# Hybrid mixer block: the delta rule's front moved to the end of its own turn, its levels spread, the first convolution tap on ScalarE

## The reference, cut to what matters

```python
qkv = jax.nn.silu(causal_depthwise_conv(concat([dq, dk_, dv_]), dn_conv_w))   # 4 taps per channel
q = l2_normalize(cq) * DN_KEY_DIM ** -0.5;  k = l2_normalize(ck);  v = cv
decay = exp(where(causal, gcum[..., :, None] - gcum[..., None, :], -inf))
a_mat = einsum('bnhid,bnhjd->bnhij', k_beta, k) * decay * strict
sol = triangular_solve(eye + a_mat, [v * beta, k_beta * exp(gcum)])            # unit lower triangular
qk = einsum('bnhid,bnhjd->bnhij', q, k) * decay
# scan over chunks: v_new = u - w @ state;  o = q_dec @ state + qk @ v_new;  state = state * d + k_dec^T @ v_new
o_dn = rms_norm(o) * gain * silu(z)
```

## Time and profile before

| | |
|---|---|
| median of three runs | 1932.82 us |
| time of the profiled execution | 1932.75 us |
| its span | 1930.9 us |
| busy: PE, PEld, DVE, ACT, POOL | 99%, 83%, 66%, 53%, 3% |
| granted TensorE clock, mean | 0.998 of full speed |

### The profile page before, as it was taken

How to read it: one execution, slowest core, us unless ns; L and a number is a source line. 1 busy time by engine, 2 the same in 40 slices (tenths; PEclk the granted TensorE clock), 3 DMA queues, 4 the chain that set the end, 5 groups by cost and what they waited for, 6 DMA issues and landing times.

```text
span 1930.9 us, 27778 instructions
## 1 busy us (share of the span) xinstructions
PE 1908.9 (99%) x9545; PEld 1607.1 (83%) x9545; DVE 1273.1 (66%) x2261; ACT 1023.4 (53%) x2068; POOL 49.6 (3%) x80
## 2 busy tenths in 40 slices
PE   9999999999999999999999999999999999999997
PEld 7888888888888888888888788888888888888886
DVE  6658888888888756565665786555555555555555
ACT  4446665666566655455444554545444444444443
POOL 1000000000000000000000000000000000000000
PEclk9999999999999999999999999999999999999999
DMA  8666555455535557566566456555565565655552
GB/s 315 207 159 190 135 136 136 132 129 132 145 117 129 181 173 245 195 202 202 189 236 206 153 198 197 194 192 182 191 196 185 186 195 181 226 202 196 196 194 89
DMA packets 204178, 349.62 MB, mean 181 GB/s; under 512 B 6768, under 2 KB 73024, under 8 KB 203088
## 3 DMA queue, kind: packets, MB, share of 16 engines
q1 hardware_dynamic: 200704, 334.00, 52.6%
q0 software_dynamic: 3264, 14.47, 4.7%
q10 hardware_dynamic: 144, 0.26, 0.0%
HBM read 344.32 MB, written 2.10 MB: 179 GB/s over the span
## 4 chain that ended last, share of the span: by engine, by line
PE 89%; DVE 5%; issue 2%; ACT 2%; DMA 1%; DVEq 0%; ACTq 0%; POOL 0%; SPq 0%; POOLq 0%
PE dense L602 23%; PE dense L604 23%; PE dense L603 23%; PE dense L590 8%; PE dense L592 4%; PE chain L760 1%; DVE lo L1422 1%; DMA raw<-in_w_in_dram 1%; PE chain L842 1%; ACT hi L1077 1%; PE chain L1027 0%; PE chain L852 0%; PE chain L719 0%; PE chain L860 0%; DVE AT L1680 0%
## 5 line engine op out<-in xcount | busy, mean ns | idle before, releaser
L1422 DVE TENSOR_TENSOR lo<-raw,hi 128x512 fp32r<-128x512 f32 x1252 | 849.2, 690 | 518.9 <-ACT hi L1077 516.5
L1077 ACT ACTIVATE hi<-raw 128x512 fp32r<-128x512 f32 x1252 | 773.2, 630 | 620.2 <-PE dense L604 596.9
L602 PE MATMUL dense<-hi,xs 128*128 128x512 f32 x1376 | 539.7, 392 | 1.7 <-DVE xs L1970 1.1
L604 PE MATMUL dense<-lo,xs 128*128 128x512 f32 x1376 | 535.9, 389 | 0.0
L603 PE MATMUL dense<-hi,xs 128*128 128x512 f32 x1376 | 535.5, 389 | 0.0
L590 PE MATMUL dense<-xs,hi 128*128 128x512 f32 x1024 | 380.3, 410 | 1.0
L602 PEld LDWEIGHTS dense<-hi,xs 128*128 128x128 f32 x1376 | 258.4, 188 | 55.3 <-DVE xs L1970 2.0
L604 PEld LDWEIGHTS dense<-lo,xs 128*128 128x128 f32 x1376 | 258.3, 188 | 54.2
L603 PEld LDWEIGHTS dense<-hi,xs 128*128 128x128 f32 x1376 | 258.5, 188 | 52.4
L592 PE MATMUL dense<-xs,lo 128*128 128x256 f32 x1024 | 286.3, 280 | 0.0
L590 PEld LDWEIGHTS dense<-xs,hi 128*128 128x128 f32 x1024 | 192.6, 188 | 44.4 <-issue 5.2
(11 more groups left out here) (317 smaller groups left out, 1435.9 us busy)
## 6 DMA issues: line engine op xcount, KB each, us to landing
raw<-in_w_in_dram SPq DMA_DIRECT2D x115, 1024.0 KB, 5.1
raw<-in_w_ffn_gate_dram SPq DMA_DIRECT2D x44, 1024.0 KB, 5.0
raw<-in_w_ffn_up_dram SPq DMA_DIRECT2D x44, 1024.0 KB, 5.0
raw<-in_w_ffn_down_dram SPq DMA_DIRECT2D x44, 1024.0 KB, 5.0
raw<-in_w_br_att_dram SPq DMA_DIRECT2D x16, 1024.0 KB, 5.2
raw<-in_w_br_dn_dram SPq DMA_DIRECT2D x16, 1024.0 KB, 5.0
raw<-in_w_out_dram SPq DMA_DIRECT2D x16, 1024.0 KB, 5.1
raw<-in_w_ple_gate_dram SPq DMA_DIRECT2D x16, 1024.0 KB, 5.0
```

The costliest lines, as they stand in the source:

```text
L602: pe.matmul(o, ah, hi[:, s, :], start=(k == 0), stop=False)
L604: mm = pe.matmul(o, ah, lo[:, s, :], start=False, stop=(k == nk - 1))
L1077: act.activation(parts(pos, n)[0], raw[:, slot, off:off + 512], ACT.Copy).then_inc(sem("hi_ready"), 1)
L1422: dve.tensor_tensor(wl, raw[:, slot, off:off + 512], wh.bitcast(F32), ALU.subtract).then_inc(sem("lo_ready"), 1)
```

## The change

Four things change.

1. **The front.** `k_to_rows` and `kk` of pair i move on TensorE from steps 1 and 0 of the next turn to steps 28 and 29 of turn i. With them go the squares of k (ScalarE, step 29, now written to `w`), the key's scale (VectorE, step 30), `AT` and `kd` (VectorE, step 31) and the packing of the blocks (ScalarE, step 31). Silu of q is at steps 18 and 19, silu of k at 25 and 26. The causal add moves from VectorE to GpSimd, behind the DMAs of the decays, and the exponential of the decays from step 31 to 12. ScalarE's wait for `on` moves to the end of the turn. `qk` stays at step 0 and waits for `ATc`.
2. **The levels** have a table of their own. Level 0 goes from step 7 to 2, levels 1 to 3 from 9, 11 and 13 to 4, 6 and 8, level 4 from 15 to 11, level 5 from 17 to 13, the last y and x products from 19 and 20 to 15 and 16.
3. **The scan** moves one step ahead, from 21 to 25 to 20 to 24, with what follows it.
4. **The first tap** of the convolution is made by ScalarE (`first_tap`, steps 10, 18 and 26, a copy with a scale per partition); VectorE starts at the second.

The semaphores of the attention's transposes are merged (`p_turned`, `p_cols`), with the same order.

```diff
+STAGE = {0: 0, 1: 1, 2: 2, 3: 3, 6: 4, 7: 5, 8: 6, 10: 8, 20: 18, 21: 19, 22: 20, 23: 21, 24: 22, 25: 23, 28: 26, 29: 27}
+LEVEL = {0: FIRST, 2: 5, 4: 7, 6: 9, 8: 11, 11: 13, 12: 14, 13: 15, 15: 16, 16: 17}
...
-    return k if k < 4 else k - 3 if k >= 19 else k - 2 if 6 <= k < 18 else FIRST if k == 5 else None
+    return STAGE.get(k)
+def level_at(k):
+    return LEVEL.get(k)
...
+            def causal(p):
+                pool.wait_ge(sem("G_in"), 32 * p + 32)
+                if p:
+                    pool.wait_ge(sem("ATc"), p)
+                    pool.wait_ge(sem("QKm"), p)
+                pool.tensor_tensor(Em[:], G[:], four(cst[:, C_CAUSAL:C_CAUSAL + P]), ALU.add).then_inc(sem("am"), 1)
...
+                    pool.wait_ge(sem("egb"), p + 1)
                     pool.wait_ge(sem("am"), p + 1)
-                    pool.wait_ge(sem("egb"), p + 1)
                     decay_in(p + 1)
+                    causal(p + 1)
...
-            def kk_qk(p):
-                pe.wait_ge(sem("silk"), p + 1)
-                if not isinstance(p, int) or p:
-                    pe.wait_ge(sem("on"), p)
+            def kk(p):
...
-                pe.wait_ge(sem("am"), p + 1)
+                pe.wait_ge(sem("ATc"), p + 1)
...
             def k_to_rows(p):
+                pe.wait_ge(sem("silk"), p + 1)
...
+                    pe.wait_ge(sem("beside"), p + 1)
...
+            def key_stage(k, i):
+                if k == 28:
+                    k_to_rows(i)
+                elif k == 29:
+                    kk(i)
...
                     cols_quarter(pos, k, k % 8, 2 * ((s + 1) % 2))
+                    key_stage(k, i)
                     if chain:
                         chain_stage(stage_at(k), i - 1, True)
+                        level_stage(level_at(k), i - 1)
                     att_stage(k - ATT_LAG, i, chain)
...
+            def first_tap(i, s):
+                act.wait_ge(sem("joined"), 4 * i + s + 1)
+                for f in range(2):
+                    act.activation((cq, ck, cv)[s][:, f, :], pad[:, f, 0:T], ACT.Copy,
+                                   scale=cw[:, 0, ds(16 * s + f + 2 * i, 1)]).then_inc(sem("first_tap"), 1)
...
+                if k == 12:
                     act.wait_ge(sem("am"), i + 1)
...
+                elif k == 18:
+                    act.wait_ge(sem("conv0"), 2 * i + 2)
+                    act.activation(flat(tmp[:]), flat(cq[:]), ACT.Tanh, scale=0.5).then_inc(sem("tanh"), 1)
+                elif k == 25:
+                    act.wait_ge(sem("conv1"), 2 * i + 2)
+                    act.activation(flat(AT[:]), flat(ck[:]), ACT.Tanh, scale=0.5).then_inc(sem("tanh"), 1)
+                elif k == 29:
+                    act.wait_ge(sem("k_rows"), i + 1)
+                    for x in range(4):
+                        r = act.activation(w[:, x // 2, x % 2, :], C[:, 2, x * P:x * P + P], ACT.Square,
+                                           accum_out=row[:, 0, x:x + 1])
+                    r.then_inc(sem("k_sum"), 1)
+                elif k == 31:
+                    if isinstance(i, int):
+                        act.wait_ge(sem("y_zero"), 1)
+                    act.wait_ge(sem("ATc"), i + 1)
+                    for q in range(4):
+                        R = quadrant(q)
+                        r = act.activation(VU[R, 0], AT[R, :, R], ACT.Copy)
+                    r.then_inc(sem("packed"), 1)
+                    for q in range(0, 4, 2):
+                        r = act.activation(VU[quadrant(q), 1], AT[quadrant(q), :, quadrant(q + 1)], ACT.Copy, scale=-1.0)
+                    r.then_inc(sem("beside"), 1)
...
                     if chain:
                         chain_k(stage_at(k), i - 1)
-                        if k == 31:
-                            act.wait_ge(sem("on"), i)
                     if k in (9, 17, 25):
                         pad_in(i, k // 8 - 1)
+                    elif k in (10, 18, 26):
+                        first_tap(i, k // 8 - 1)
                     att_k(k - ATT_LAG, i)
                     qk_front(k, i)
                     if chain:
-                        inverse_k(stage_at(k), i - 1)
+                        inverse_k(level_at(k), i - 1)
+                if chain:
+                    act.wait_ge(sem("on"), i)
...
+                if j == 0:
+                    return
...
+                if j == 1:
+                    dve.wait_ge(sem("first_tap"), 6 * i + 2 * s + f + 1)
...
+                if k in (19, 26):
+                    n = (19, 26).index(k)
+                    th, dst, name = ((tmp, cq, "silq"), (AT, ck, "silk"))[n]
...
+                elif k == 30:
+                    dve.wait_ge(sem("k_sum"), i + 1)
+                    dve.tensor_scalar(row[:, 1, :], row[:, 0, :], 4 * L2_EPS, None, ALU.add).then_inc(sem("k_eps"), 1)
...
+                elif k == 31:
+                    dve.wait_ge(sem("KK"), i + 1)
+                    dve.wait_ge(sem("E"), i + 1)
+                    dve.wait_ge(sem("b_scale"), i + 1)
...
+                    a.then_inc(sem("ATc"), 1)
...
+                        chain_k(level_at(k), i - 1)
                         chain_k(stage_at(k), i - 1)
```

More of the change, by code:

```diff
@@ L540, in _ @@
             unit_blocks(0)
+            causal(0)
             for p in range(PAIRS):
@@ L1172, in chain_k @@
                 elif k == 1:
-                    act.wait_ge(sem("k_rows"), p + 1)
-                    for x in range(4):
-                        r = act.activation(tmp[:, x, :], C[:, 2, x * P:x * P + P], ACT.Square, accum_out=row[:, 0, x:x + 1])
-                    r.then_inc(sem("k_sum"), 1)
                     act.wait_ge(sem("G_in"), 32 * p + 32)
@@ L1182, in chain_k @@
                     act.activation(k1[:], ck[:, :, P:T], ACT.Copy).then_inc(sem("k1"), 1)
-                elif k == 14:
-                    act.wait_ge(sem("vu_out"), nth("vu_out", 4, p))
-                    for q in range(4):
-                        R = quadrant(q)
-                        act.activation(Um[R, :, R], VU[R, 2], ACT.Copy)
-                elif k == 3:
-                    act.wait_ge(sem("ATc"), p + 1)
-                    for q in range(4):
-                        R = quadrant(q)
-                        r = act.activation(VU[R, 0], AT[R, :, R], ACT.Copy)
-                    for q in range(0, 4, 2):
-                        r = act.activation(VU[quadrant(q), 1], AT[quadrant(q), :, quadrant(q + 1)], ACT.Copy, scale=-1.0)
-                    r.then_inc(sem("packed"), 1)
+                elif k == 3:
                     act.wait_ge(sem("v_rows"), p + 1)
@@ L1220, in chain_k @@
                     act.wait_ge(sem("silz"), p + 1)
+                    if not isinstance(p, int):
+                        act.wait_ge(sem("silq"), p + 2)
                     for h in range(2):
@@ L1235, in inverse_k @@
                                    ACT.Copy).then_inc(sem("vu_out"), 1)
+                elif k == 14:
+                    act.wait_ge(sem("vu_out"), nth("vu_out", 4, p))
+                    for q in range(4):
+                        R = quadrant(q)
+                        act.activation(Um[R, :, R], VU[R, 2], ACT.Copy)
                 elif k == 15:
@@ L1611, in qk_front @@
                     dve.scalar_tensor_tensor(flat(dst[:]), flat(th[:]), 1.0, flat(dst[:]), ALU.add,
                                              ALU.mult).then_inc(sem(name), 1)
-                elif k == 29:
-                    dve.wait_ge(sem("G_in"), 32 * i + 32)
-                    dve.wait_ge(sem("silq"), i + 1)
-                    dve.tensor_tensor(Em[:], G[:], four(cst[:, C_CAUSAL:C_CAUSAL + P]), ALU.add).then_inc(sem("am"), 1)
+                elif k == 30:
+                    dve.wait_ge(sem("k_sum"), i + 1)
+                    dve.tensor_scalar(row[:, 1, :], row[:, 0, :], 4 * L2_EPS, None, ALU.add).then_inc(sem("k_eps"), 1)
+                    dve.wait_ge(sem("k_eps"), i + 1)
+                    dve.reciprocal(row[:, 3, :], row[:, 1, :]).then_inc(sem("k_inv"), 1)
+                    dve.wait_ge(sem("k_inv"), i + 1)
+                    dve.tensor_tensor(by_head(row[:, 2, :]), per_pair(beta, i), by_head(row[:, 3, :]),
+                                      ALU.mult).then_inc(sem("b_scale"), 1)
+                elif k == 31:
+                    dve.wait_ge(sem("KK"), i + 1)
+                    dve.wait_ge(sem("E"), i + 1)
+                    dve.wait_ge(sem("b_scale"), i + 1)
+                    for x in range(4):
+                        a = dve.scalar_tensor_tensor(out=AT[:, x, :], in0=C[:, 0, P * x:P * x + P], scalar=row[:, 2, x:x + 1],
+                                                     in1=Em[:, x, :], op0=ALU.mult, op1=ALU.mult)
+                    a.then_inc(sem("ATc"), 1)
+                    dve.tensor_tensor(kd[:], C[:, 2, :].rearrange("p (h t c) -> p h t c", h=2, t=TT)[:, :, 0, :],
+                                      each(kdecs[:, 0, ds(2 * i, 2)], 2), ALU.mult).then_inc(sem("kdec"), 1)
```

82 lines of the change are left out of this document (26 added, 56 removed).

## The result

| | before | changed |
|---|---|---|
| median | 1932.93 us (4 runs, 1932.26 to 1934.65) | 1954.10 us (4 runs, 1953.49 to 1955.44) |
| profiled execution, its span | 1932.75, 1930.9 | 1953.49, 1951.7 |
| granted TensorE clock, mean | 0.998 | 0.995 |
| loop turn (turns 2 to 7) | 65.0 | 67.6 to 68.8 |

The change makes the kernel slower: ratio 1.0109, 95% interval 1.0092 to 1.0127, that is 21.2 us by the medians. The forecast was 1942.4 us and a range up to 1951.0: the direction and the places of the new waits were right, the size was less than half of the measured one. A full turn of the loop took 67.6 to 68.8 us; the forecast said 66.4.

A forecast was written before the change was run, and what follows sets the result against it. TensorE, busy 99% of the span, was taken as the bound, so only its waits count. Against 1932.75 us, -13.6 + 11.2 + 2 + 4 + 6 = +9.6 gave 1942.4 us; range 1929 to 1951 (forecast's own 1936 to 1949).

The forecast's parts named there:

- What goes: Waits for `on` (5.1 us), level zero's wait and slow group (7.5), two fewer breaks per turn (1.0): together -13.6 us.
- Last level: Steps 11 to 16: `Yz` ready at 12.1 us, TensorE there at 10.49; stall 1.6 per turn, 11.2 us in all.
- The next turn's start: Six turns: silu of v makes v to rows late by 1.2, taken as 1.0 per turn; 6 us (0 to 9).
- Scan: Steps 21 to 23: state copy behind rotation 0.5 late, `rhs` 0.2 late again; 4 us in all (0 to 9).
- attention's turns: Steps 16 and 17: probabilities late behind the last level's work in VectorE's queue; 2 us in all (0 to 6).
- Rival 1 and 2: 1: queues keep up, 1923 to 1927 us, chance 0.12; 2: only the last level stalls, 1931 to 1934 us, 0.20.
- Rival 1: Slack in VectorE's and ScalarE's queues shrinks new waits: -13.6 and at most 4 back, say 1924 us; chance 0.12.
- Rival 3: GpSimd's add holds VectorE for its length, `sE` and `ATc` late too: 1950 to 1956 us; chance 0.08.
- Rival 4: Wait for `on` only becomes one for `silk` at step 28: up to 3 us back; chance counted within the forecast's.

The follow-up runs named there:

- exp_late: The changed kernel with ScalarE's four exponentials of the decay moved from step 12 to step 22; 1947.1 us.
- v_rows_back: transpose_first with v to rows put back to its place in the changed kernel; 1932.5 us.
- rotation_back: transpose_first with VectorE's rotation and copies of keys and values back at steps 20 and 21; 1924.6 us.
- transpose_first: Changed kernel with levels spread later, v to rows a quarter later, rotation and keys at 23/24, decay's exponentials at 22, Tm's last transpose before the convolution's join; 1924.0 us.
- causal_on_vector: The changed kernel with the causal add on VectorE at step 10 instead of GpSimd; 1955.9 us.
- rotation_late: The changed kernel with VectorE's rotation and copy of keys and values moved from steps 20 and 21 to 23 and 24; 1954.6 us.
- v_rows_late: The changed kernel with v to rows one quarter later; 1954.0 us.
- tap_on_vector: The changed kernel with the convolution's first tap back on VectorE at its old place in the queue; 1955.9 us.
- exp_and_last_level_late: The changed kernel with the decay's exponentials at step 22 and the last level's products at steps 16 and 18; 1955.8 us.
- last_level_late: The changed kernel with the last level's two products moved from steps 15 and 16 to 16 and 18; 1955.3 us.
- exp_and_v_rows: The changed kernel with the decay's exponentials at step 22 and v to rows one quarter later; 1943.3 us.

## Why the forecast was half of the loss

The paths were right. What failed is the price of what becomes late, in four terms: the clock (3.3 us, in no term of the sum), v to rows (9.8 instead of 6), the last level's product (14.1 instead of 11.2), and some 2 us of small waits that no term has. The figures are TensorE's starts in the two profiles, over the loop: how late a group starts, plus how much longer than undisturbed it takes until the next one.

**What goes.** Right in kind, a little less in size. The two old waits (4.1 for `on`, 3.1 for level zero, by starts) and the slower groups behind them (1.2 and 3.3) were 11.7 us, and next to nothing of them is left. With the 1.0 for two fewer breaks per turn, which no run prices alone, that is 12.7 for the forecast 13.6. No run has the moved front without the rest either, so this term is read from the traces only. The front at the end of its turn and `ATc` were in time: `qk` starts 13.9 us behind scan_o (372.04 to 385.92), by the count 13.75.

**Last level.** The mechanism and the path were right to 0.2: TensorE there after 10.5 us (counted 10.49), `Yz` written 12.2 after level four's start (counted 12.05), stall 1.72 to 1.77 in the seven turns (1.6), 12.2 us in all. What failed is the price of a stall. The prediction says that a group which had to be waited for costs its wait and nearly 0.5 more, and books that for level zero, which goes (3.3 us), but not for the new waits. The last level's product takes 1.01 us until the next group, and 1.15 and 1.35 in two of the turns in which the clock fell, against 0.81 in the kernel before: 1.9 us. With it the place costs 14.1 instead of 11.2. ScalarE's part of the path was overrated (1.19 for the exponentials, 0.6 by exp_late), which did not matter for the sum since VectorE's queue was 0.6 behind.

**The next turn's start.** Due at 17.45 by the count and at 17.7 in the trace, silu of v 16.5 behind o_eps (16.2): again right, and then spoiled by the taker. I computed 1.2, took 1.0 "since the sum has over twenty pieces", and six turns. The chain runs in seven turns of the loop; the group is 1.33 to 1.38 late in six of them and 0.80 in the first, and takes 0.14 longer each time: 9.8 for the forecast 6, and 8.5 when priced alone (v_rows_back).

**Scan, attention's turns.** By starts 4.7 more than before (forecast 4) and 2.4 (forecast 2). But the scan's term is hardly a loss of its own: rotation_back puts its 4.6 us of waits back into transpose_first and the time moves by 0.7, since silk is waited for less.

**What was missing.** The clock: 3.3 us, in no term and no rival. The earlier trace rows and the mean clock of 0.998 told only that it had not fallen in the loop before; its longest stalls there are 0.9 us, and I put a wait of 1.6 into every turn without asking what TensorE's clock would do. And some 2 us of small waits and slower groups at `qk`, k to rows and q to rows.

The steps come to -12.7 + 14.1 + 9.8 + 4.7 + 2.4 + 3.3 + 2.0 = 23.6 us by starts in the profile; measured are 21.2, and the spans differ by 20.8. The 2 to 3 us between stay open: terms overlap (a fall also lengthens the groups that are counted with the waits, and the wait for `sO` behind it is gone), and I can't separate them.

**Rivals.** Rival 1 and 2 are out by the first rows. (Rival 1's own sum, -13.6 and at most 4 back, gives 1919 to 1923 and not 1923 to 1927.) Rival 3 has the right size (1950 to 1956) for a wrong reason: the add on GpSimd takes 1.59 us on average, but causal_on_vector shows it costs nothing, and `ATc` was in time. Rival 4 came about in small: `kk` does not wait, and k to rows waits 1.3 us in all for silk.

How far the add and the splits hold each other is in these rows of the changed kernel, GpSimd's and then VectorE's:

```profile
469.62 1.69 POOL L551 TENSOR_TENSOR Em<-G,cst 128x512 f32<-128x512 f32 x1 [10.15 <-DMA G<-grow]
```

```profile
469.49 0.69 DVE L1468 TENSOR_TENSOR lo<-raw,hi 128x512 fp32r<-128x512 f32 x1
470.93 0.94 DVE L1468 TENSOR_TENSOR lo<-raw,hi 128x512 fp32r<-128x512 f32 x1 [0.76 <-ACT hi L1107]
```

The add begins inside the first split and ends 1.15 behind that split's end (470.17 to 471.32). The second split begins inside the add and ends 0.55 behind the add's end, so it takes 0.94 instead of 0.69. Both distances are the same in all seven full turns. In the first turn no split is ahead of the add: it takes 1.27, and the split that begins 0.28 behind it takes 1.54, again to 0.55 behind the add's end. So one waits for the other; it is not a slowdown of both. A split in a full turn pays only 0.25 because VectorE came to it late, 0.76 us idle behind ScalarE's part of the split. This agrees with what the Trainium skill (GPSIMD Engine Reference, section 1, Specifications) says of contention between GpSimd and Vector instructions with two SBUF inputs. The same page's 4497 ns for an add of 2048 columns (section 3) would make this one 1.1 us, by estimate. The trace has 1.27 undisturbed, and 1.56 to 1.69 where a split was ahead.

What stays open: why the clock falls behind some gaps and not others of the same size. In the changed kernel gaps of 1.84 to 1.89 us had three falls in seven, in causal_on_vector the same gaps had four, in rotation_late five, in v_rows_late six; in tap_on_vector 1.76 to 1.82 had two, in exp_and_last_level_late 1.94 to 2.02 had five, in last_level_late 2.55 to 2.62 only two. Ahead of the loop the kernel before has a gap of 2.16 us (42.8) and transpose_first one of 2.68 (43.8), both without a fall. No fall came behind a gap of 1.5 or less, in any of these profiles. Each profile is one execution, though the mean clocks of the other runs go with it. One run of exp_and_v_rows took 1947.2 us at 0.996, the other four 1942.8 to 1943.5 at 0.998 and 0.999; what its clock did, no profile shows.

## What to carry to other kernels

Price a new wait as you price one that goes: its length, the slow group behind it, in every turn, and not rounded down. When an engine's queue is late, look for all its outputs: moving one consumer can let another meet the same lateness (`sE` for `Yz`, level zero for v to rows), while taking an instruction from ahead of it in that queue (0.69 us of a join ahead of a 0.31 us transpose) gave 4.7 us. Before an edit that puts a stall of the size seen here into a loop, add the clock as a term, and read the granted clock's stretches first in any experiment that comes out at nothing: here v to rows a quarter later gained nothing until the long gap was gone.

## What the runs showed of the hardware

A single gap of some 1.8 us in a turn in which TensorE is otherwise busy was in some turns enough for a stretch of 3.4 us at 1.2 GHz (three of seven in the changed kernel); each one cost about 1.1 us of time. Behind gaps of 1.5 us or less there was none. A GpSimd add of 128x512 and VectorE's splits of the same size waited for each other: the add took 1.27 us with no split ahead of it and ended 1.15 behind a split that was; a split that began inside the add ended 0.55 behind its end (935 to 937 ns, once 1540, instead of 685). TensorE's waits at `Yz`, `cv` and `S` were the same with the add on VectorE.
